# Hyena convolution of a two-block transformer: time split into four classes instead of two, filter spectra computed one step ahead

## The reference, cut to what matters

```python
h = h @ w3.astype(f32)
h = h.reshape(L, 2, HY_ORDER, D) * decay[:, None, None, :]
fwd, bwd = h[:, 0], h[:, 1]
k = jnp.concatenate([fwd, jnp.zeros((1, HY_ORDER, D), f32), bwd[1:][::-1]], axis=0)
k = k / jnp.sum(jnp.abs(k), axis=0, keepdims=True)
...
for o, gate in enumerate((x1, x2)):
    z = gate.astype(f32) * (long_conv(z, kf[:, o]) + fbias[o].astype(f32) * z)
return z.astype(xn.dtype) @ w_out + b_out
```

## Time and profile before

| | us |
|---|---|
| median of three runs | 4454.34 |
| lowest, highest run | 4445.87, 4467.5 |
| span of the profiled execution | 4437.2 |
| PE busy | 4169.9 (94%) |
| DVE busy | 2225.3 (50%) |
| POOL busy | 1445.5 (33%) |
| ACT busy | 1236.0 (28%) |

### The profile page before, as it was taken

One profiled execution on the slowest core, in us unless ns is written; L12 is line 12 of the kernel. 1 busy time (PEld: TensorE's weight loads), 2 busy tenths in 40 slices (PEclk: granted clock), 3 DMA queues, 4 the chain that ended last, 5 costly groups with the idle time before them and its releaser, 6 DMA issues.

```text
span 4437.2 us, 48379 instructions
## 1 busy us (share of the span) xinstructions
PE 4169.9 (94%) x19126; PEld 3108.9 (70%) x19126; DVE 2225.3 (50%) x3267; ACT 1236.0 (28%) x1725; POOL 1445.5 (33%) x834
## 2 busy tenths in 40 slices
PE   7999999999999699999999999989998999998999
PEld 6656888656788488877557887566666666685887
DVE  6567435365424652465774444556663357404322
ACT  3322212135222322233233222322322224422221
POOL 3311344200344144434123442357574000231343
PEclk9999999999999899999999998989999879999999
DMA  6200232210232123221003222121212121221232
GB/s 181 76 16 23 111 105 88 105 48 28 101 115 77 70 96 118 81 77 67 28 29 131 99 90 68 43 60 31 60 30 57 59 77 60 74 95 62 90 105 76
DMA packets 96913, 333.75 MB, mean 75 GB/s; under 512 B 44336, under 2 KB 47536, under 8 KB 67888
## 3 DMA queue, kind: packets, MB, share of 16 engines
q1 hardware_dynamic: 87968, 311.85, 20.2%
q10 hardware_dynamic: 8720, 18.82, 1.7%
HBM read 317.53 MB, written 13.11 MB: 75 GB/s over the span
## 4 chain that ended last, share of the span: by engine, by line
PE 80%; DVE 14%; ACT 2%; POOL 2%; issue 1%; DMA 0%; SPq 0%; DVEq 0%; ACTq 0%; POOLq 0%
PE bank L903 16%; PE bank L904 16%; PE bank L905 16%; PE bank L1340 5%; PE bank L867 4%; PE bank L1107 3%; PE bank L1057 2%; PE bank L1320 1%; PE bank L1641 1%; PE bank L1081 1%; PE bank L1640 1%; PE bank L1662 1%; PE bank L1572 1%; PE bank L1601 1%; DVE work L2598 1%
## 5 line engine op out<-in xcount | busy, mean ns | idle before, releaser
L782 POOL TENSOR_TENSOR w_lo<-ring,w_hi 128x2048 fp32r<-128x2048 f32 (+2 forms) x200 | 777.2, 3886 | 1509.6 <-ACT w_hi L1777 1483.1
L903 PE MATMUL bank<-x_hi,w_hi 128*128 128x512 f32 x1584 | 618.2, 390 | 7.5 <-POOL w_lo L782 7.5
L905 PE MATMUL bank<-x_hi,w_lo 128*128 128x512 f32 x1584 | 616.9, 389 | 0.0
L904 PE MATMUL bank<-x_lo,w_hi 128*128 128x512 f32 x1584 | 616.7, 389 | 0.0
L1777 ACT ACTIVATE w_hi<-ring 128x2048 fp32r<-128x2048 f32 (+2 forms) x200 | 322.0, 1610 | 712.8 <-PE bank L905 711.9
L903 PE MATMUL bank<-h_hi,w_hi 128*128 128x512 f32 x960 | 373.9, 389 | 0.4
L904 PE MATMUL bank<-h_lo,w_hi 128*128 128x512 f32 x960 | 373.5, 389 | 0.0
L905 PE MATMUL bank<-h_hi,w_lo 128*128 128x512 f32 x960 | 373.4, 389 | 0.0
L903 PEld LDWEIGHTS bank<-x_hi,w_hi 128*128 128x128 f32 x1584 | 297.8, 188 | 70.6 <-POOL w_lo L782 9.2
L905 PEld LDWEIGHTS bank<-x_hi,w_lo 128*128 128x128 f32 x1584 | 297.6, 188 | 62.1
L904 PEld LDWEIGHTS bank<-x_lo,w_hi 128*128 128x128 f32 x1584 | 297.8, 188 | 61.5
(11 more groups left out here) (468 smaller groups left out, 7666.1 us busy)
## 6 DMA issues: line engine op xcount, KB each, us to landing
ring<-stream SPq DMA_DIRECT2D x212, 1024.0 KB, 4.8
ring<-stream SPq DMA_DIRECT2D x64, 704.0 KB, 4.0
ring<-stream SPq DMA_DIRECT2D x36, 512.0 KB, 3.6
xn<-first_mods SPq DMA_DIRECT2D x8, 1024.0 KB, 6.9
ring<-stream SPq DMA_DIRECT2D x4, 1088.0 KB, 5.0
bias_rows<-work ACTq DMA_DIRECT2D x1, 4096.0 KB, 46.4
work<-bias_rows ACTq DMA_DIRECT2D x1, 3072.0 KB, 11.2
tab<-tabs ACTq DMA_DIRECT2D x1, 2624.0 KB, 16.8
```

What stands on the lines that cost most here:

```text
L782: nc.gpsimd.tensor_tensor(w_lo[:, j % 2, 0:cols], ring[:, k % RING, 0:cols], w_hi[:, j % 2, 0:cols], ALU.subtract).then_inc(wlo_set, 1)
L903: mm(b[:], hi[:, at + k, :], rhs_hi, start=(k == 0), stop=False)
L904: mm(b[:], hi[:, at + k, :], rhs_lo[:, k, :], start=False, stop=False)
L905: ins = mm(b[:], lo[:, at + k, :], rhs_hi, start=False, stop=(k == kt - 1))
```

## The change

The change rewrites the four steps.

- **Four classes.** Times are split by their remainder r modulo 4 (`hy[..., r:T:4]`), 128 of each. Each signal tile is one matmul instead of two (8 instead of 16 a step). The filter keeps 16, since its forward and backward parts use other sign combinations. The inverse takes 32 matmuls of 128 columns instead of 256. The sums and differences over the classes, which the matmuls did before, are made by DVE: `four_classes` in front of the product and `folded` behind it. The sine inputs are sorted by class, so that the taps read them without a stride.
- **Filter spectra a step ahead.** There are two buffers (`K = (xn, spectrum2)`). The whole next spectrum, its magnitudes and the next signal's transposes stand ahead of the inverse on PE, and `filter_pair` is spread between the parts of the product on DVE. The taps stand directly before the inverse in steps 0 and 1; steps 2 and 3 have none.
- **x is parked.** The magnitudes of both filter halves are taken by ACT (two `Abs`) into the space of `x`, and DVE needs one maximum instead of two operations. ACT issues a DMA that writes `x` (2 MB) to `x_keep` at j = 18 of the input projection and one that brings it back in step 3.
- **POOL waits.** The decays for steps 1 and 2 wait for the second `prod_set` of steps 0 and 1, the low weights of the output projection for those of steps 2 and 3.
- **Last step.** DVE works on 256 columns at a time (two parts), and `low_z(0..3)` stands behind both parts instead of ahead of the step; `first_half` on PE waits for it as before.

The core of the diff:

```diff
+        mags, mags2 = x[:, 0:4, :], x[:, 4:8, :]
+        partner = ctmp.rearrange("p a b c -> p (a b) c")
+        cross = TB("cross").rearrange("p (g c) -> p g c", g=3)
+        cross3 = kbuf2[:, 0:512].unsqueeze(1)
...
-        K = xn
+        K = (xn, spectrum2)
...
+                decay(0)
+                decay(1)
+                for i in range(2):
+                    pool.wait_ge(prod_set, 10 * n["hyena"] + 2 * (i + 1))
+                    decay(i + 2)
+                pool.wait_ge(prod_set, 10 * n["hyena"] + 6)
+                for b in range(2):
                     low_weights(first + 18 + b, out_hi[b])
+                pool.wait_ge(prod_set, 10 * n["hyena"] + 10)
+                for b in range(2, 4):
+                    low_weights(first + 18 + b, out_hi[b])
+                n["hyena"] += 1
...
+                def signal_spectra():
+                    for t in range(n["turned"] - 4, n["turned"]):
+                        pe.wait_ge(aux_drained[aux.place(t)], aux.turn(t) + 1)
+                    for pair in SIGNAL_PAIRS:
+                        for kind, r in pair:
+                            mm(open_aux()[:], fwd[kind, r, 1], u_tm[:, r, :], start=True, stop=True).then_inc(aux_full, 1)
...
+                def inverse(tiles_of, full_, cts):
+                    tiles = [tiles_of() for _ in cts]
+                    pe.wait_ge(prod_set, n["prod"] + 1)
+                    for b, ct in zip(tiles, cts):
+                        inverse_tile(b, ct, 0)
+                        inverse_tile(b, ct, 2)
+                    pe.wait_ge(prod_set, n["prod"] + 2)
+                    for b, ct in zip(tiles, cts):
+                        inverse_tile(b, ct, 1)
+                        inverse_tile(b, ct, 3).then_inc(full_, 1)
+                    n["prod"] += 2
...
                 pe.wait_ge(conv_done, 24 * (s + 1))
+                turns(0)
                 for i in range(4):
-                    o, c = i // 2, i % 2
-                    if i == 1:
-                        pe.wait_ge(*taps[1][0])
+                    signal_spectra()
                     if i < 3:
-                        taps_of((i + 1) % 2, taps[0] if i == 0 else taps[1][1])
-
...
-                        spectra(lambda kind: filt[:, kind], (0,))
+                        filter_spectra(FILTER_PAIRS[:3])
+                        turns(i + 1)
+                        filter_pairs(FILTER_PAIRS[3:])
+                        magnitudes()
                     else:
                         begun = first_half(0) + first_half(1)
...
+                    if i == 0:
+                        pe.wait_ge(*later[0])
+                    if i < 2:
+                        taps_of(i, later[1])
                     if i < 3:
-                        spectra(lambda kind: filt[:, kind], (1,))
-                        magnitudes()
+                        inverse(open_acc, acc_full, range(4))
+                    else:
+                        inverse(open_aux, aux_full, range(2))
+                        inverse(open_aux, aux_full, range(2, 4))
...
+                    signal(go(mags2, filt[:, 1], ACT.Abs), abs_set)
...
+                    if j == 18:
+                        act.dma_start(x_keep.rearrange("(k p) t -> p k t", p=P), x[:]).then_inc(hy_x_out, 16)
...
+                        magnitudes()
+                        spectra(3)
+                        turned()
+                        spectra(1)
+                        aux.n += 1
+                    if i == 3:
+                        act.dma_start(x[:], x_keep.rearrange("(k p) t -> p k t", p=P)).then_inc(hy_x_back, 16)
+                    if i == 2:
+                        for j in range(2):
+                            high_weights(starts[("hyena", s)] + 18 + j, out_hi[j])
                     if i == 3:
                         for m in range(4):
                             high_z(m)
-                    spectra(4)
+                        act.wait_ge(aux_full, aux.n)
+                        high_weights(starts[("hyena", s)] + 20, out_hi[2])
+                    for ct in range(2):
+                        scaled_rows(i, ct)
+                    if i < 2:
+                        taps()
...
-                    n["abs"] += 1
+                    n["abs"] += 2
                     dve.wait_ge(abs_set, n["abs"])
-                    step(stt(mags, filt[:, 1], -1.0, mags, ALU.mult, ALU.max))
-                    signal(tt_(mags, filt[:, 1], mags, ALU.max), mags_set)
+                    signal(tt_(mags, mags, mags2, ALU.max), mags_set)
...
+                    c = i % 2
+                    next_ = K[1 - c] if i < 3 else None
+                    signal_pair(0, U[:, 0, :], U[:, 2, :])
+                    signal_pair(1, U[:, 1, :], U[:, 3, :])
+                    signal_pair(2, partner[:, 0, :], partner[:, 3, :])
+                    signal_pair(3, partner[:, 1, :], partner[:, 2, :], True)
                     if i < 3:
+                        whole = slice(0, 512)
+                        four_classes(whole)
+                        filter_pair(next_, 0)
+                        crossed(K[c], whole)
+                        filter_pair(next_, 1)
+                        magnitudes()
+                        straight(K[c], whole)
+                        filter_pair(next_, 2)
+                        joined(whole)
+                        aux.n += 4
+                        folded(whole)
+                        filter_pair(next_, 3)
+                        norms(1 - c)
+                    else:
+                        for part in (slice(0, 256), slice(256, 512)):
+                            four_classes(part)
+                            crossed(K[c], part)
+                            straight(K[c], part)
+                            joined(part)
+                            folded(part)
+                    if i < 2:
                         acc.n += 8
-                    aux.n += 4
                     if i == 3:
                         for m in range(4):
                             low_z(m)
...
+                        y = bank(t, i == 3)[:].rearrange("c (r h) -> c h r", r=4)
+                        drain(stt(mid, y, invn[:, m:m + 1], mid, ALU.mult, ALU.add), t, i == 3)
+                        signal(tt_(z, zbias[:, ct % 2, :], hy[:, 8 * (i // 2) + m, :], ALU.mult), gated)
...
+                dve.wait_ge(hy_x_back, 16 * (s + 1))
...
+            def four_classes(cs):
+
+                tt_(U[:, 4:8, cs], U[:, 0:4, cs], partner[:, :, cs], ALU.subtract)
+                step(tt_(U[:, 0:4, cs], U[:, 0:4, cs], partner[:, :, cs], ALU.add))
+
+            def crossed(ker, cs):
+
+                tt_(partner[:, :, cs], U[:, 1:8:2, cs], ker[:, 1:8:2, cs], ALU.mult)
+                tt_(cross[:, :, cs], U[:, 0:6:2, cs], ker[:, 1:7:2, cs], ALU.mult)
+                step(tt_(cross3[:, :, cs], U[:, 6:7, cs], ker[:, 7:8, cs], ALU.mult))
+
+            def straight(ker, cs):
+
+                tt_(U[:, 0:8:2, cs], U[:, 0:8:2, cs], ker[:, 0:8:2, cs], ALU.mult)
+                step(tt_(U[:, 1:8:2, cs], U[:, 1:8:2, cs], ker[:, 0:8:2, cs], ALU.mult))
+
+            def joined(cs):
+
+                tt_(U[:, 0:8:2, cs], U[:, 0:8:2, cs], partner[:, :, cs], ALU.subtract)
+                tt_(U[:, 1:7:2, cs], U[:, 1:7:2, cs], cross[:, :, cs], ALU.add)
+                step(tt_(U[:, 7:8, cs], U[:, 7:8, cs], cross3[:, :, cs], ALU.add))
+
+            def folded(cs):
+
+                low, high = U[:, 0:4, cs], U[:, 4:8, cs]
+                step(tt_(high, low, high, ALU.subtract))
+                step(stt(low, low, 2.0, high, ALU.mult, ALU.subtract))
+                first, second = U[:, 0:2, cs], U[:, 2:4, cs]
+                step(tt_(second, first, second, ALU.subtract))
+                signal(stt(first, first, 2.0, second, ALU.mult, ALU.subtract), prod_set)
+                first, second = U[:, 4:6, cs], U[:, 7:5:-1, cs]
+                step(tt_(second, first, second, ALU.subtract))
+                signal(stt(first, first, 2.0, second, ALU.mult, ALU.subtract), prod_set)
```

263 lines of the change are left out of this document (110 added, 153 removed).

## The result

| | before | after |
|---|---|---|
| median of 20 runs | 4455.6 | 4465.2 |
| lowest, highest run | 4442.6, 4467.5 | 4457.6, 4473.4 |
| device time of the profiled execution | not listed | 4464.3 |
| its span | 4437.2 | 4462.5 |

After takes 1.0025 times as long as before (95% interval 1.0015 to 1.0034): 10 us more, where 11 were forecast. The time fell on the forecast, but not every term did. The two profiled executions lie 25 us apart. That of before lies under its median (by about 17 us), that of after on it (1 us under).

A forecast was written before the change was run, and what follows sets the result against it. DVE becomes the bound, with waits between it and PE: three steps shrink by 7 us and the last gives it back, 5.4 later a layer, +11 in two, span 4448, plus 17: 4465 us, range 4425 to 4505.

The forecast's parts named there:

- DVE work, PE savings, prices: Per step: DVE work 46 us; PE saves 7.0 us of spectrum and 8.8 of inverse; inverse records cost 0.112 each.
- Steps 0 and 1, 54.5: Steps 0 and 1, zero to zero: 54.5 us each (53.5 warm, 57 colder), with PE later than DVE before the inverse.
- bank wait: Steps 0 and 1: PE's fourth tile of transposes waits for pair 2's bank, which DVE reads out at 20.0.
- I take 2.5: PE resuming at the lower clock after a wait: 1.7 to 3.5 us, taken as 2.5, paid once in a step.
- POOL and the gates: Decays end at 43.8 in steps 0 and 1, first gate ends at 44.5; in step 2 POOL's low weights delay two gates.
- The last step, 69.9: Last step: PE waits for the low parts behind DVE's product, `first_half` and inverses queue behind; ends at 69.9 us (66.5 to 74).
- The sum: All steps: 450.0 against 444.6, 5.4 us later a layer; two layers +11 us, span 4448, median 4465.
- the median lies 17 above it: Whole kernel: the median lies 17 us above the profiled execution's 4437.2, carried over from span 4448 to median 4465.
- The clock rival: PE's clock stays low after its waits: 62 us a layer, 4589; a third of that 4506; chance 0.27 in part or whole.
- The mild form by the Trainium skill's rule: Each of three PE resumptions in a step starts cold: 20 us a layer more, making the change a loss of 51 us.
- DVE-bound: Banks, taps and POOL cost nothing: steps of 47.2 us, 4412; chance 0.15 together with whatever else was made too dear.
- That POOL doesn't hold DVE: Step 2 is 48.5 us, the last 65: 436.3, 8 a layer less, 4438; counted within the main case's 0.58.

The follow-up runs named there:

- the pair of shortened products: Two runs on the changed kernel: steps 0 to 2 without the three operations joining straight and crossed products, 4451.3 us; without two of three crossed products, 4444.0 us.
- the run without joins: Changed kernel, DVE's product in steps 0 to 2 without the three operations that join straight and crossed products: 4451.3 us, ratio 0.9995.
- the pieces: Changed kernel, POOL forms the low parts of the output weight blocks in four operations of 512 columns instead of one of 2048: 4448.5 us, ratio 0.9995.
- the run without waits: Changed kernel with POOL's four waits for the sums of products removed: 4470.6 us, ratio 1.0042.

## Why the prediction was right, and where it wasn't

- **DVE work, PE savings, prices.** Right: DVE 46.1 us in steps 0 and 1 (46 forecast), inverse records at 0.113, sums at +31.7 and +34.2 (31.8, 34.3), transposes at +20.0.
- **Steps 0 and 1, 54.5.** Right in layer 3 (54.3, 54.4), and by its own chain, as the pair of shortened products shows: bank wait, magnitudes, taps, inverse. The term that was mis-sized is "I take 2.5" for the clock, paid once: 2.3 in layer 3 (the fourth transposes and filter pair 3 cold), and in step 1 of layer 0 3.8 us more, where magnitudes and taps were cold as well. It needed a spread over executions, not one price; in five profiles the steps lie 0.8 us above 54.3 on average, 4.0 at most.
- **POOL and the gates.** Steps 0 and 1 as forecast: the decays ended at +43.6 (43.8) and the gate's first half began at +43.7 (43.0), so none was held. In step 2 POOL held one gate, not two, because the inverse ran cold (9.40 us for 64 records) and the first half of the first gate ended at +39.5 instead of 37.5, when POOL was already in its second block. Two errors of opposite sign, and the step is right (55.7, 56.6).
- **The last step, 69.9.** Right (70.6 and 69.9 to the last record) and for the reason given: with the low parts ahead of the product it is 17 us shorter (14 net, since they then stand in the step ahead of it). Also right that `low_z(0)` runs ahead of POOL: four take 7.07, 0.69 plus 4.5 of POOL and three more. By the rule of the Trainium skill (SBUF — State Buffer, "SBUF: two separate sides"), that the first to start holds the shared port for its whole instruction, the trace agrees: POOL's block, begun 0.04 us behind it, took 5.02 instead of 4.5, and without its waits POOL and DVE alternate in whole instructions.
- **The sum.** The forecast put 5.4 us on each layer and nothing elsewhere, a span of 4448; the profile has 4462.5, 14.5 more. Layer 0 grew by 11.0, layer 3 by 8.8, and the rest by 5.4, where the change touches nothing and two profiles of before differ by 7. So the change in the two layers was put at half of what the profiles show. The base of layer 3 is part of it: "layer 3 has the same step to 0.1 us, so one layer is worked out and doubled" holds for steps 0 to 2 (61.5, 61.5, 54.5 in both), not for the last step. PE's spectra at its start, before, in layer 0 and in layer 3:

```profile
385.02 16.27 PE L1107 MATMUL bank<-work,tab 128*128 128x512 f32 x32 [0.95 <-ACT work L1920]
...
2285.91 13.97 PE L1107 MATMUL bank<-work,tab 128*128 128x512 f32 x32 [1.40 <-ACT work L1920]
```

In layer 0 they began cold, and there a layer took 237.3 us and not 234.8. That the median still fell on 4465 is because "the median lies 17 above it" held for before and not for after (2.7): two errors that cancel, and that is luck. What can be compared is the difference of the medians, 10 for my 11, and part of that is luck too, since the profiles put 20 us into the two stretches.

- **Rivals.** The clock rival didn't come: 0.2 to 3.8 us more a step in layer 0, at most 1.1 in layer 3, and no gain from keeping PE busy in the bank wait. The mild form by the Trainium skill's rule (TensorE: Matmul & The Clock Gate, "HAM oscillation — how this bites in real kernels"), every burst between waits cold at 20 us a layer, came in part (the page tells it of bursts that are shorter than the waits between them; here they are mostly longer): the clock of a step is 0.71 to 0.91 where it was 0.91 to 0.97, and the last 6 records of signal spectrum run cold in several runs; but layer 0 paid 5 us for it in steps 0 and 1 beyond the forecast, and layer 3 nothing. DVE-bound: refuted for steps 0 and 1 by the run without joins; step 2 does follow DVE. That POOL doesn't hold DVE: refuted by the pieces and by the run without waits. Its sum was off, too: with steps 0 and 1 at 54.5, 48.5 and 65 end at 438.1 and not 436.3, which is 4441, still no change.
